# Two transformer blocks on one core: the first block's norms taken at the evacuation, its input transposed unscaled, and each weight group in two transfers

## The reference, cut to what matters

```python
def first_block(x, ...):                     # one layer
    u = rmsnorm(h, norm_mix_g)               # h = x
    proj = u @ w_in                          # 2048 x 4096: Fourier part, q, k, v
    y = concat(fourier_mix(proj[:1024]), dilated_attention(q, k, v))
    h = h + y @ w_out                        # 2048 x 2048
    u = rmsnorm(h, norm_mlp_g)
    a = square(relu(u @ w_up))               # 2048 x 8192
    h = h + a @ w_down                       # 8192 x 2048
    return rmsnorm(h, norm_final_g)

# rmsnorm(x, g) = x * rsqrt(mean(x*x) + eps) * g   (one factor per token, one per channel)
# second block: modulated norms, gated linear attention and convolution,
# output projection, then a gated feed-forward network; w_mod (2048 x 12288) makes its modulation
```

## Time and profile before

| | us |
|---|---|
| median of 3 runs | 2426.72 (2421.72 to 2428.9) |
| the profiled execution | 2423.29 |
| its span, first to last instruction | 2421.6 |
| outside the span | 1.7 |
| PE busy | 2337.5 |
| DVE busy | 1558.3 |
| ACT busy | 1083.1 |
| weight transfers of 1 MB on SP | 384, and 4 of 128 KB |

### The profile page before, as it was taken

How to read it: one execution, slowest core, us unless ns; L and a number is a source line. 1 busy time by engine, 2 the same in 40 slices (tenths; PEclk the granted TensorE clock), 3 DMA queues, 4 the chain that set the end, 5 groups by cost and what they waited for, 6 DMA issues and landing times.

```text
span 2421.6 us, 28456 instructions
## 1 busy us (share of the span) xinstructions
PE 2337.5 (97%) x10667; PEld 1917.2 (79%) x10667; DVE 1558.3 (64%) x1837; ACT 1083.1 (45%) x1267; POOL 145.0 (6%) x210
## 2 busy tenths in 40 slices
PE   7999898999999999998999999998999999999997
PEld 5887787888888888887777877786888888888886
DVE  6886456877877876876767845556444554455555
ACT  5434345444444444443573363444444344434443
POOL 1110000111111111110000100000000000000000
PEclk9999899999999999999999999998999999999999
DMA  9884255988888888884856654353655665556552
GB/s 316 280 270 156 67 193 182 314 302 266 281 283 270 281 277 268 278 282 165 296 188 216 208 178 136 125 188 124 206 191 185 195 210 187 190 190 196 190 177 104
DMA packets 238209, 521.51 MB, mean 215 GB/s; under 512 B 13712, under 2 KB 13840, under 8 KB 236816
## 3 DMA queue, kind: packets, MB, share of 16 engines
q1 hardware_dynamic: 208000, 405.30, 51.4%
q0 software_dynamic: 29248, 109.85, 13.4%
q10 hardware_dynamic: 848, 4.85, 0.5%
HBM read 515.77 MB, written 4.19 MB: 215 GB/s over the span
## 4 chain that ended last, share of the span: by engine, by line
PE 93%; DVE 4%; ACT 1%; issue 1%; DMA 1%; DVEq 0%; SPq 0%; ACTq 0%
PE acc L1312 28%; PE acc L1314 28%; PE acc L1313 28%; PE tp L1327 2%; PE m L1337 1%; DVE wlo L823 1%; DVE macc L843 1%; PE tp L1571 1%; PE acc L1392 1%; DMA mring<-w_mod 1%; PE m L1402 0%; DMA h<-x 0%; PE m L1537 0%; PE tp L1589 0%; PE tp L1583 0%
## 5 line engine op out<-in xcount | busy, mean ns | idle before, releaser
L452 ACT ACTIVATE whi<-wring 128x1024 fp32r<-128x1024 f32 x776 | 813.7, 1052 | 1143.2 <-PE acc L1314 1140.0
L823 DVE TENSOR_TENSOR wlo<-wring,whi 128x1024 fp32r<-128x1024 f32 x776 | 935.7, 1214 | 602.0 <-ACT whi L452 597.9
L1312 PE MATMUL acc<-whi,xhi 128*128 128x512 f32 x2208 | 876.1, 397 | 6.8 <-DVE xlo L979 3.4
L1313 PE MATMUL acc<-wlo,xhi 128*128 128x512 f32 x2208 | 865.8, 392 | 0.0
L1314 PE MATMUL acc<-whi,xlo 128*128 128x512 f32 x2208 | 865.3, 392 | 0.0
L1312 PEld LDWEIGHTS acc<-whi,xhi 128*128 128x128 f32 x2208 | 418.9, 190 | 103.4 <-issue 12.8
L1314 PEld LDWEIGHTS acc<-whi,xlo 128*128 128x128 f32 x2208 | 418.4, 190 | 88.7
L1313 PEld LDWEIGHTS acc<-wlo,xhi 128*128 128x128 f32 x2208 | 418.9, 190 | 85.7 <-issue 1.0
L843 DVE SCALAR_TENSOR_TENSOR macc<-mring,csil,macc 128x512 f32<-128x512 f32 x480 | 344.2, 748 | 33.4 <-DMA mring<-w_mod 22.0
L403 POOL DMA_DIRECT2D mring<-w_mod x192 | 136.4, 711 | 1211.5 <-DVE macc L843 1191.8
L1312 PE MATMUL acc<-whi,ahi 128*128 128x512 f32 x512 | 200.9, 392 | 0.0
(11 more groups left out here) (189 smaller groups left out, 1082.6 us busy)
## 6 DMA issues: line engine op xcount, KB each, us to landing
wring<-w_up SPq DMA_DIRECT2D x108, 1024.0 KB, 5.6
wring<-w_down SPq DMA_DIRECT2D x108, 1024.0 KB, 5.4
mring<-w_mod POOLq DMA_DIRECT2D x192, 512.0 KB, 5.2
wring<-w_in SPq DMA_DIRECT2D x92, 1024.0 KB, 5.8
wring<-w_gate SPq DMA_DIRECT2D x44, 1024.0 KB, 5.2
wring<-w_out SPq DMA_DIRECT2D x32, 1024.0 KB, 5.1
h<-x SPq DMA_DIRECT2D x4, 512.0 KB, 7.4
gbig<-ctx_in POOLq DMA_DIRECT2D x2, 1024.0 KB, 7.8
```

The lines of the kernel that those rows point to most:

```text
L452: act.activation(whi[:, piece_slot(c, piece), 0:half], wring[:, g4, piece * half:(piece + 1) * half], ACT.Copy).then_inc(hi_done, 1)
L823: dve.tensor_tensor(wlo[:, h4, 0:half], wring[:, g4, piece * half:(piece + 1) * half], whi[:, h4, 0:half].bitcast(F32), ALU.subtract).then ...
L1312: pe.matmul(dst, hi[:, tile, rows], whi[:, h4, w], start=(kg == first and k == 0), stop=False)
L1313: pe.matmul(dst, hi[:, tile, rows], wlo[:, h4, w], start=False, stop=False)
```

## The change

Five things are changed.

- **Block 1's first norm.** x is not scaled. `x_opening` turns a quarter of `h` when its piece has landed, and multiplies the quarter before; the squares of x come after group 3 has been rounded, and with them the exponential for `c`, mean, root and reciprocal. The factor is applied when ACT evacuates a block of w_in, by two instructions of 128x512, one for each half of the tokens.
- **The first loads.** SP loads only piece 0 of x and then goes on to the weights; ACT loads the identity, the vectors, pieces 1 to 3 of x, and last the other tables.
- **The MLP norm.** Quarters of `h` are turned while w_out is still multiplied (`turn_added(n - 1)` in the middle of block n, the last one after the first group of w_up) into `ahi`/`alo`; the squared activations go into `xhi`/`xlo` instead. `norm_mean(1)` and `norm_root(1)` are apart, beside groups 1 and 2 of the MLP as DVE counts them. The factor is a scale of the Relu, in all chunks, in two instructions.
- **The weights.** Each group is loaded by two transfers of half its tiles, with a semaphore for each; ACT waits for each half by itself.
- The loop over the blocks of w_out is written out for ACT and DVE.

The diff, cut to its core:

```diff
@@ load
-                sp.dma_start(dst, src).then_inc(group_landed[c.slot("g", WSLOTS)], 16)
+                half = kts // SPLIT
+                for piece in range(SPLIT):
+                    ks = slice(piece * half, (piece + 1) * half)
+                    sp.dma_start(dst[:, ks, :], src[:, ks, :]).then_inc(piece_landed[c.slot("g", WSLOTS)][piece], 16)
...
-            for piece in range(KG):
-                cols = slice(piece * NB, (piece + 1) * NB)
-                sp.dma_start(h[:, :, cols], x[:, cols].rearrange("(t p) n -> p t n", p=P)).then_inc(x_in[piece], 16)
+            sp.dma_start(h[:, :, 0:NB], x[:, 0:NB].rearrange("(t p) n -> p t n", p=P)).then_inc(x_in[0], 16)
@@ round_groups
-                    act.wait_ge(group_landed[g4], c.landed("g", WSLOTS))
                     for piece in range(SPLIT):
+                        act.wait_ge(piece_landed[g4][piece], c.landed("g", WSLOTS))
@@ ACT, opening
+            act.dma_start(tabs[:, 0, :], tables[:, 0, :]).then_inc(start_in, 16)
             act.dma_start(vrows[:, :, :], vectors).then_inc(start_in, 16)
-            act.dma_start(tabs[:, :, :], tables).then_inc(start_in, 16)
+            for piece in range(1, KG):
+                cols = slice(piece * NB, (piece + 1) * NB)
+                act.dma_start(h[:, :, cols], x[:, cols].rearrange("(t p) n -> p t n", p=P)).then_inc(x_in[piece], 16)
+            act.dma_start(tabs[:, 1:7, :], tables[:, 1:7, :]).then_inc(tabs_in, 16)
...
-            root_and_scale(0, h, u_mix)
...
                     if first and j == 0:
-                        opening(lambda b0, b1: round_banks(xhi, 2 * b0, b1 - b0,
-                                                           lambda k: vecs[:, 0, V_MIXG + k:V_MIXG + k + 1]), 1)
+                        for piece in range(KG):
+                            round_banks(xhi, 4 * piece, 2, lambda k: vecs[:, 0, V_MIXG + k:V_MIXG + k + 1])
+                            round_groups(1)
+                        for piece in range(KG):
+                            square_x(piece)
                         c_exponential()
+                        root(0)
                     else:
                         round_groups(2)
                     round_groups(2)
                     wait_block(2)
-                    act.activation(proj[:, :, bass.ds(i * (2 * NB) + j * NB, NB)], acc[:, 2 * j:2 * j + 2, :],
-                                   ACT.Copy).then_inc(proj_set, 1)
+                    if first and j == 0:
+                        act.wait_ge(rstd_done, 1)
+                    for t in range(T):
+                        last = act.activation(proj[:, t, bass.ds(i * (2 * NB) + j * NB, NB)], acc[:, 2 * j + t, :],
+                                              ACT.Copy, scale=rstd[:, 0, t:t + 1])
+                    last.then_inc(proj_set, 1)
@@ ACT, w_out and MLP
-            with c.loop(act, 2, g=8, ha=2, ssq=2 * T) as i:
-                added_pair(i)
-            root_and_scale(1, h, u_mlp)
+            round_groups(2)
+            for n in range(3):
+                round_groups(4)
+                round_added(n)
+                square_added(n * NB, n)
+            round_groups(2)
+            round_added(3)
+            square_added(3 * NB, 3)
...
+                if first:
+                    act.wait_ge(rstd_done, 2)
+                for t in range(T):
+                    last = act.activation(blk2[:, t, :], acc[:, 2 * (j % 2) + t, :], ACT.Relu, scale=rstd[:, 1, t:t + 1])
+                last.then_inc(blk_half, 1)
@@ DVE, opening
                     if first and g == 0:
-                        opening(lambda b0, b1: remain_banks(xhi, xlo, 2 * b0, b1 - b0,
-                                                            lambda k: vecs[:, 0, V_MIXG + k:V_MIXG + k + 1]), 1)
+                        for piece in range(KG):
+                            remain_banks(xhi, xlo, 4 * piece, 2, lambda k: vecs[:, 0, V_MIXG + k:V_MIXG + k + 1])
+                            remainders(1)
+                        for piece in range(KG):
+                            square_x(piece)
                         c_silu()
+                        dve.wait_ge(x_squares_a, KG)
+                        dve.wait_ge(x_squares_v, KG)
+                        norm_root(0)
@@ DVE, w_out and MLP
-            with c.loop(dve, 2, g=8) as i:
-                for pair in range(2):
-                    remainders(3)
-                    wait_block(1)
-                    add_block(i * (2 * NB) + pair * NB, pair)
-                    remainders(1)
+            for n in range(4):
+                remainders(2)
+                if n:
+                    remain_added(n - 1)
+                remainders(1)
+                wait_block(1)
+                add_block(n * NB, n % 2)
+                remainders(1)
+            remain_added(3)
             c.add("ssq", T * KG)
-            norm_scale(1, h, u_mlp)
...
+                    if first and g == 1:
+                        norm_mean(1)
+                    elif first and g == 2:
+                        norm_root(1, mean=False)
@@ PE
+            def x_opening():
+                for piece in range(KG):
+                    pe.wait_ge(x_in[piece], 16)
+                    turn_rows(h, 2, 2 * piece)
+                    if piece:
+                        multiply(xhi, xlo, (piece - 1,), 4, 0)
+                pe.wait_ge(tp_free, c.at("q", 2))
+                multiply(xhi, xlo, (KG - 1,), 4, 0)
+                pe.wait_ge(pool_set, 1)
...
                     pe.wait_ge(h_added, c.at("ha", 1))
-                    multiply(xhi, xlo, range(4), 4, n % 2)
+                    multiply(xhi, xlo, (0, 1), 4, n % 2)
+                    turn_added(n - 1)
+                    multiply(xhi, xlo, (2, 3), 4, n % 2)
                 c.add("ha")
-            pe.wait_ge(u_done, 2 * T)
...
-                    hi, lo = (xhi, xlo) if j < 4 else (ahi, alo)
+                    hi, lo = (ahi, alo) if j < 4 else (xhi, xlo)
                     for kg in range(3):
                         multiply(hi, lo, (kg,), 4, pair)
+                        if first and j == 0 and kg == 0:
+                            turn_added(3)
```

More of the change, by code:

```diff
@@ L155, in two_blocks @@
             arden = sb("arden", [P, HEADS, T], scope=ph)
-        u_mix = proj[:, :, 0:D]
         fpos = blk
@@ L164, in two_blocks @@
             alo = sb("alo", [P, KT, S], F32R, scope=ph)
-            u_mlp = sb("u_mlp", [P, T, D], scope=ph)
+            sb("ctx_place", [P, T, D], scope=ph)
             mgain = sb("mgain", [P, D], scope=ph)
@@ L202, in two_blocks @@
         hspill = nc.dram_tensor("hspill", [T, P, D], F32).ap()
-        group_landed = [sem(f"group_landed{i}") for i in range(WSLOTS)]
+        piece_landed = [[sem(f"piece_landed{i}_{piece}") for piece in range(SPLIT)] for i in range(WSLOTS)]
         hi_done = sem("hi_done")
@@ L518, in norm, with square_x @@
                 root_and_scale(n, src, dst)
+            act.dma_start(tabs[:, 0, :], tables[:, 0, :]).then_inc(start_in, 16)
             act.dma_start(vrows[:, :, :], vectors).then_inc(start_in, 16)
-            act.dma_start(tabs[:, :, :], tables).then_inc(start_in, 16)
+            for piece in range(1, KG):
+                cols = slice(piece * NB, (piece + 1) * NB)
+                act.dma_start(h[:, :, cols], x[:, cols].rearrange("(t p) n -> p t n", p=P)).then_inc(x_in[piece], 16)
+            act.dma_start(tabs[:, 1:7, :], tables[:, 1:7, :]).then_inc(tabs_in, 16)
             act.sem_inc(proj_set, 2)
-            for piece in range(KG):
+            def square_x(piece):
                 act.wait_ge(x_in[piece], 16)
@@ L528, in _ @@
                     act.wait_ge(x_squares_a, piece)
-                act.activation(acc[:, 0, :], h[:, 0, piece * NB:(piece + 1) * NB], ACT.Square,
+                act.activation(m0[:, :], h[:, 0, piece * NB:(piece + 1) * NB], ACT.Square,
                                accum_out=squares[:, 0, piece:piece + 1]).then_inc(x_squares_a, 1)
-            root_and_scale(0, h, u_mix)
             act.wait_ge(vec_set, 1)
-            round_groups(1)
             c.n["ha"] = H0
@@ L629, in mlp_chunk @@
                 for j in range(8):
+                    round_groups(1)
+                    if j >= 5:
+                        square_block(j - 5, first)
+                    round_groups(1)
                     if first and j == 0:
-                        opening(lambda b0, b1: round_banks(xhi, 2 * b0, b1 - b0,
-                                                           lambda k: vecs[:, 0, V_MLPG + k:V_MLPG + k + 1]))
-                    else:
-                        round_groups(1)
-                        if j >= 5:
-                            square_block(j - 5, first)
-                        round_groups(1)
+                        root(1)
                     if 1 <= j <= 4:
-                        round_banks(ahi, 4 * (j - 1), 2)
+                        round_banks(xhi, 4 * (j - 1), 2)
                     round_groups(2)
```

(23 more changed lines are left out.)

36 lines of the change are left out of this document (16 added, 20 removed).

## The result

The changed kernel takes **2403.11 us** (median of four runs, 2402.81 to 2403.26), the kernel before 2424.22 beside it (2421.43 to 2428.9). These two medians are 21.1 us apart. The ratio on record is 0.9903 with an interval of [0.9886, 0.9921]; it stands for a gain of 23.5 us, from 19 to 28. The forecast was 2409.4, a gain of 17.3 us. The two profiled executions have spans of 2421.6 and 2401.4 us, 20.2 apart.

What follows compares the result with a forecast made beforehand. PE was taken as the bound, busy for 97% of the span. First norm 5.4 us plus MLP norm 12.1 less evacuation 0.2 gave 17.3 us, so 2426.7 - 17.3 = 2409.4 us, range 2403 to 2416.

Steps and rivals of the forecast that it cites:

- The sign: Whole kernel: faster than before with chance 0.94, same 0.03, slower 0.03.
- the MLP norm's size: From w_out to the end of the first w_up block: a gain of 12.1 us, bounds 9 and 12.5.
- the wait for group 4: Block 1's opening: PE waits 4.0 us, with group 3 landing at 30.8 us and a table load for the exponential.
- group 50, the thinnest: First MLP block: group 50 ready about 10 us after w_out's block 3, needed after 11.7, the thinnest cover.
- The start of PE: Block 1's opening: first matmul of a weight at 11.7 us instead of 21.47, 9.8 us earlier.
- The vectors: Opening: issued at 0.89 us and landed at 5.4 us, letting PE's first quarter turn from 6.2 us.
- The slow matmuls: Opening: 8 matmuls at the lower clock against about 6 before, costing 0.4 us of the earlier start.
- the stated bound of 1.4: Wait for group 4: at least 1.4 us if group 3 is in time and only the chain counts.
- the first half: Block 1's first norm: 9.4 us from the earlier start less 4.0 of waiting, net 5.4 us, from 2 to 8.3.
- rival 1: Opening: no wait at group 4, group 3 landing earlier or exponential needing no table; gain 21.3 us, 2405.5; chance 0.20.
- Evacuation: Two instructions of 512 for one of 1024: 0.2 us lost where the attention starts, between 0 and 0.4.
- The split: Halved weight transfers: can only matter in the opening, saving nothing in the middle of the run.

Runs made afterwards that it cites:

- e9: The changed kernel again, word for word, in more executions: 2404.25 us.
- e2: The kernel before with only the first norm's part and the first loads of the change (1 MB transfers, MLP norm as before): 2416.5 us.
- e4: The changed kernel without the split, weights loaded by 1 MB transfers again: 2405.56 us.
- e5: The changed kernel with one tiny unused Copy on ACT ahead of the wait for the vectors, taking the table load off the opening: 2403.2 us.
- e7: The changed kernel with POOL's loads of the attention's tables and first w_mod steps released by piece 0 of x, not piece 3: 2409.13 us.
- e6: The changed kernel with each piece's squares right behind the rounding of its group, not all behind group 3: 2402.07 us.
- e8: The changed kernel with both e5's early table load and e6's squares beside the quarters: 2400.74 us.
- e1: The kernel before with only the split, each weight group loaded by two 512 KB transfers: ratio 0.9998, median 2423.59 us.
- e11: e8 with unused transposes keeping PE busy in three openings of the second block, as in e10: 2398.04 us.
- e10: The kernel before with unused transposes filling PE's waits at the second block's first two openings and at the last norm: 2419.84 us.
- e3: The kernel before with only the MLP norm's part of the change (1 MB transfers, opening as before): 2411.43 us.

## Why the prediction was right or wrong

The sign, the order of the two parts and the MLP norm's size were right. The total was 3 us short in the traces (20.2 against 17.3), and 6 us short in the median (2403.1 against 2409.4). The step that failed is the wait for group 4 (point 3): 4.0 us were forecast and 0.6 came, because the forecast started its chain at a landing of group 3 at 30.8 us, and in the run it starts behind PE's own turn at 27.2 us. Step by step:

1. **The MLP norm** was forecast at 12.1 us. The table goes from 6.0 to 18.1 at this place: 12.1. No cover broke, and group 50, the thinnest, came in time. What the step left out is 1.0 us further on: before, DVE had to wait for the data of w_mod behind the pause and was late with its sums. Its timeline, before:

```profile
405.37 1.54 DVE L843 SCALAR_TENSOR_TENSOR macc<-mring,csil,macc 128x512 f32<-128x512 f32 x2 [2.45 <-DMA mring<-w_mod]
```

   That PE then waited 0.8 us for them could be read in the view of PE's waits. I looked for the longest waits there and not at the short one behind the norm.

2. **The start of PE** was forecast 9.8 us earlier and came 7.8 earlier (8.2 in the second trace, e9). Two terms were mis-sized. The vectors: I took the landing of before, 5.4 us; but the changed kernel issues them second, behind the identity. ACT's timeline, after:

```profile
0.89 0.45 ACTq L522 DMA_DIRECT2D tabs<-tables  x1
1.37 0.49 ACTq L523 DMA_DIRECT2D vrows<-vectors  x1
```

   Issued 0.5 us later and with more beside them, they were there at 6.66, and at 6.1 to 6.3 in e2 and e4 to e9. PE's first turn began at 7.36 and not at 6.2. And ACT's table load was missing in the sum. In the kernel before, it lay in time in which ACT had nothing to do (from 1.97 us on, while x was still to come); taking the squares away from there moved it onto the path. e5 shows this term by itself: from the first turn to the first matmul of a weight PE needs 6.27 us in the changed kernel (7.36 to 13.63) and 5.05 in e5 (6.94 to 11.99), where the forecast had 5.5. The slow matmuls cost what they were forecast to (24 matmuls in 7.19 us, 1.7 more than 24 x 0.227). This half gave 7.4 at the end of group 0, not 9.4.

3. **The wait for group 4** was forecast at 4.0 us and measured at 0.6, below even the stated bound of 1.4. This is the step with the largest error, and it hid the one in step 2: that the first half came out near its forecast (6.3 against 5.2) is luck.

   What failed first is where the chain begins. I started it when group 3 lands, at 30.8 us, and wrote that "the bytes ahead of it are the same ones". It landed at 25.5. The bytes ahead of it were not the same: the last piece of x came 4.3 us later, and with it POOL's 3.4 MB, as the prediction says under rival 1. ACT then didn't wait for group 3 at all. It rounded it behind the last quarter of x, for which it had waited for PE's turn. So the chain hangs on PE: in e5 PE is 1.6 to 1.8 us earlier throughout the opening, and the wait is 0.59 us again. That PE came to group 4 at 39.1, 2.5 us behind the forecast's 36.6, is therefore not what made the wait short. e7 shows that the landing would have mattered, had it been late: with POOL's transfers early ACT waits for weights, and PE's wait is 2.1 us.

   What failed second is a term of the chain. The exponential has no table load of its own; in the kernel before, the load ahead of it was needed only because the root had come before it. That is 1.28 us that I charged to ACT. Not all of it is saved, since DVE's mean ended the chain: ACT stood idle for 1.32 us ahead of the root. From ACT's last rounding of group 3 to the end of the root it took 6.1 us (31.15 to 37.27), where the forecast had 6.4.

   Rival 1, "no wait at group 4", describes this half better than the forecast, and gives both of these reasons; its total of 2405.5 comes nearer too. But its gain of 9.4 us didn't come, only 7.4 less 0.9 for the wait and what surrounds it, less 0.2 at the evacuation.

4. **Evacuation**: 0.2 us forecast, 0.24 measured (2.30 less 2.06 us of waiting for `proj`). The attention then starts on a slow stretch:

```profile
200.64 5.29 PE L1436 MATMUL acc<-tab_f,proj 128*128 128x512 f32 x8
```

   Before, eight of the same took 3.60 us. The clock is 0.66 from 200 to 205 us after, and 1.00 from 206 to 211 in the kernel before. At 310 us the gain is back at 6.3, because the attention behind this stretch has fewer slow matmuls after (17 against 27). e2 has the same program up to this place as e4 and no slow stretch here (clock 1.00 from 200 to 205), while e4, e5 and e9 have it, and e6 to e8 don't. So it isn't fixed by the change of the first norm; whether anything in the change makes it more likely is open.

5. **The split** saves nothing in the middle and costs nothing (e1), as forecast; at the start I expected the halves to matter and they don't (e4). By the Trainium skill, "DMA: Bandwidth & Descriptors", section on measured bandwidth, transfers should have at least 1 MiB to reach three quarters of the peak. No run here shows a loss from 512 KB ones that are queued behind each other; the share stays 0.84 in e1. By the Trainium skill, "ScalarE: Activation LUTs", section on the cost of a table load, a change of set costs about 2.7 us with draining. In the kernel before, where ACT is busy on both sides of a load, it takes 1.31 us from the end of the rounding (38.66) to the start of the exponential (39.97), and taking the load out of the opening gives 1.1 to 1.3 us (e5), so the traces don't bear out the longer figure.

6. **From the traces to the median.** I set the forecast's gain against the median of before. The profiled execution of before is a fast one of its kernel: 2423.29 where e1 to e11 ran beside medians of 2425.6 to 2427.3, while that of after lies at the median of its own (2403.11). So some 3 us of the 23.5 that the ratio gives are the choice of the execution. The kernel before has more places at which the clock falls; with e10 filling three of them it gets 3 to 8 us faster. That slow stretches are a cost of each wait, beyond the first one, wasn't in the sum for any stage but the one where PE's wait was taken away.

So the 2.9 us between the traces' 20.2 and the forecast's 17.3 are: start -2.0, wait +3.4, the rest up to the attention and w_out -0.6 (0.3 of it the matmuls around the wait), the sums of w_mod +1.0, and +1.0 in the second block and behind it, in stages that are the same in both kernels and differ in slow matmuls (the sum is off by 0.1 from rounding).

**Left open**: what decides how many matmuls are slow in one execution (the attention had 15 to 27 of them in kernels that don't differ there), why the opening's first matmuls are slow at a clock of 1.00 in the rows, and whether filling the attention's waits would narrow the spread.

## What to carry to other kernels

When a step is moved away from a place, ask what else it did there: the squares had hidden ACT's table load, and the old order of transfers had set when the vectors came. A new wait should be costed with the landing times of the new issue order, of every queue, and with the table set that the engine has loaded by then; here both errors were larger than the wait itself. Look, too, for what a chain starts with: if it is the waiting engine's own earlier work, the chain moves along when that engine gets faster, and the wait stays. And where PE has to wait anyway, a few transposes whose result isn't used can keep its clock up: 2.7 us on e8, 3 to 8 us on the kernel before.

## What the runs showed of the hardware

- **A wait of PE costs more than its length.** In the changed kernel the turn behind the 7.67 us wait takes 1.97 us; in e11, behind 62 transposes and a wait of 0.91 us, it takes 1.09. The clock granted after the pause is the lower of its two levels (0.50 of 2.4 GHz from 1640 to 1653 us in e8, and 1.00 from 1640 to 1645 in e11).
- **The time of one program spreads with the granted clock, by some us.** The kernel before takes 2420.7 to 2421.2 us in runs with a mean clock of 0.986 and 2428.8 to 2429.8 with 0.982 or 0.983. The count of slow matmuls in a stage isn't fixed by the stage: the same attention has 27 in the kernel before, 17 in both traces of the changed kernel and 15 in e3.
- **A transfer's landing depends on what the other queues have under way, also when they issue behind it.** Group 3's last half, issued at 7.0 us, landed 18.5 us later with POOL's 3.4 MB asked for from 15.73 us on. In e7, with these asked for from 5.98 us on, weights issued at 4.5 to 7.0 us took 21.3 to 24.0 us.
